# A hybrid RG-LRU and Gated DeltaNet step: one z tile's matmuls moved between front-stage steps, key loads and buffers rearranged, and a column group placed ahead of the RG-LRU gate products

## The reference, cut to what matters

```python
hn = rmsnorm(x, norm1)
xr, yr, qkv_raw, z, rest = jnp.split(hn @ w_in, SPLITS)
xc = causal_conv(xr) + rg_conv_b
gate_r = sigmoid(blockwise(xc, w_a) + b_a); gate_i = sigmoid(blockwise(xc, w_i) + b_i)
h = scan(a, sqrt(1 - a * a) * gate_i * xc)      # a from gate_r
out_rg = gelu(yr) * h
q, k, v = split(silu(causal_conv(qkv_raw)))      # q, k normalised
# per chunk of 128 tokens and head: A = 1 + strict(beta * k k^T * decay), solved for u, w
o, S = gated_delta_chunked(q, k, v, g, beta, S0)
out_gdn = rmsnorm(o, gdn_norm_w) * silu(z)
x = x + concat(out_rg, out_gdn) @ w_out
x = x + (silu(rms(x) @ w_gate) * (rms(x) @ w_up)) @ w_down
```

## Time and profile before

| | |
|---|---|
| median of 3 runs | 1476.22 us (1474.85 to 1478.69) |
| profiled execution: its time | 1474.63 us |
| its span in the trace | 1472.8 us |
| PE busy | 1416.4 us, 96% of the span |
| DVE, ACT, POOL busy | 42%, 25%, 11% |
| a q, k, v store of 512 KB, issue to landing (median) | 2.7 us |

### The profile page before, as it was taken

The page is one execution under the profiler, slowest core; times in us unless marked ns, Lnnn a source line. Parts: engine busy times, 40 slices in busy tenths (PEclk is TensorE's granted clock), DMA queues, the critical chain, the costliest instruction groups (busy, mean ns, idle before and its releaser), DMA issues.

```text
span 1472.8 us, 20785 instructions
## 1 busy us (share of the span) xinstructions
PE 1416.4 (96%) x8140; PEld 1299.6 (88%) x8140; DVE 625.5 (42%) x929; ACT 373.3 (25%) x612; POOL 158.6 (11%) x251
## 2 busy tenths in 40 slices
PE   6999999998898999999999999999999999999997
PEld 6888899997786899889898989898989898989895
DVE  6365455533352666643424242424242424242416
ACT  5345544332251222122020202020202020202012
POOL 3000000105474222210000000000000000000001
PEclk9999999997999999999999999999999999999999
DMA  6102211243544444327110101010101010100003
GB/s 224 62 18 75 75 69 74 100 145 133 194 173 126 140 129 126 123 99 283 54 58 29 57 28 57 28 57 28 57 28 57 28 57 28 57 28 28 0 0 121
DMA packets 66810, 119.93 MB, mean 81 GB/s; under 512 B 14672, under 2 KB 40208, under 8 KB 66768
## 3 DMA queue, kind: packets, MB, share of 16 engines
q1 hardware_dynamic: 66768, 119.36, 23.7%
HBM read 90.00 MB, written 29.34 MB: 81 GB/s over the span
## 4 chain that ended last, share of the span: by engine, by line
PE 46%; issue 2%; DMA 2%; ACT 2%; DVE 1%; SPq 0%; POOL 0%; ACTq 0%; DVEq 0%; POOLq 0%
PE bank L92 16%; PE bank L94 15%; PE bank L93 15%; ACT gu_hi L2060 1%; DMA gu_first_raw<-in_w_up 1%; DMA out_y<-y_out 1%; DVE acc L2146 0%; DVE y_out L2110 0%; DVE hf L2122 0%; ACT y_out L2096 0%; SPq L1987 0%; ACT gu_first_hi L2060 0%; SPq L1983 0%; POOL fstat L2161 0%; ACTq L81 0%
## 5 line engine op out<-in xcount | busy, mean ns | idle before, releaser
L92 PE MATMUL bank<-ht_hi,w_hi 128*128 128x364 f32 (+1 forms) x576 | 191.5, 332 | 0.0
L94 PE MATMUL bank<-ht_hi,w_lo 128*128 128x364 f32 (+1 forms) x576 | 189.9, 330 | 0.0
L93 PE MATMUL bank<-ht_lo,w_hi 128*128 128x364 f32 (+1 forms) x576 | 189.8, 330 | 0.0
L2122 DVE TENSOR_TENSOR hf<-sg,bank 128x364 f32<-128x364 f32 (+1 forms) x66 | 35.1, 532 | 338.6 <-PE bank L94 335.3
L92 PE MATMUL bank<-ht_hi,gu_hi 128*128 128x364 f32 (+1 forms) x528 | 173.2, 328 | 0.9 <-DVE hf L2122 0.9
L92 PE MATMUL bank<-ht_hi,gu_first_hi 128*128 128x364 f32 (+1 forms) x528 | 173.6, 329 | 0.5 <-PEq L930 0.5
L94 PE MATMUL bank<-ht_hi,gu_first_lo 128*128 128x364 f32 (+1 forms) x528 | 173.5, 329 | 0.0
L93 PE MATMUL bank<-ht_lo,gu_first_hi 128*128 128x364 f32 (+1 forms) x528 | 173.4, 328 | 0.0
L93 PE MATMUL bank<-ht_lo,gu_hi 128*128 128x364 f32 (+1 forms) x528 | 173.1, 328 | 0.0
L94 PE MATMUL bank<-ht_hi,gu_lo 128*128 128x364 f32 (+1 forms) x528 | 173.1, 328 | 0.0
L2146 DVE TENSOR_TENSOR acc<-acc,bank 128x512 f32<-128x512 f32 (+1 forms) x198 | 132.3, 685 | 90.3 <-PE bank L94 90.3
(11 more groups left out here) (297 smaller groups left out, 2213.5 us busy)
## 6 DMA issues: line engine op xcount, KB each, us to landing
w_raw<-in_w_in SPq DMA_DIRECT2D x24, 512.0 KB, 4.4
dn_raw<-in_w_down SPq DMA_DIRECT2D x22, 512.0 KB, 4.3
scratch_qkv<-cb_y SPq DMA_DIRECT2D x12, 512.0 KB, 2.7
scratch_kept<-kept SPq DMA_DIRECT2D x8, 768.0 KB, 3.7
gu_first_raw<-in_w_gate SPq DMA_DIRECT2D x11, 512.0 KB, 3.5
gu_first_raw<-in_w_up SPq DMA_DIRECT2D x11, 512.0 KB, 4.4
gu_raw<-in_w_gate SPq DMA_DIRECT2D x11, 512.0 KB, 3.5
gu_raw<-in_w_up SPq DMA_DIRECT2D x11, 512.0 KB, 4.4
```

Of the source, the lines that this page charges most:

```text
L92: pe.matmul(out, w_hi, x_hi, start=start, stop=False)
L93: pe.matmul(out, w_hi, x_lo, start=False, stop=False)
L94: return pe.matmul(out, w_lo, x_hi, start=False, stop=stop)
L2122: eng.tensor_tensor(hf[b][:, 0:m], sg[b][:, 0:m], psum[2 * b + 1][:, 0:m], ALU.mult).then_inc(hf_done, 1)
```

## The change

Five edits, in which TZ+1 is "the third z tile" by the new order of work.

1. PE projects only z tile TZ in the input block. Tile TZ+1 is made in the front stage, one step of three matmuls at a time (`z1_step`), at three places per front: ahead of `front`, behind it, and ahead of `products`. 24 steps fill fronts 0 to 7. Each of its three column groups uses bank 7; ACT copies it out (`keep_z1`) in fronts 2, 4 and 7, and the next group's first step waits for that copy. SP stores the row in front 7, and the load of `sub_u` waits for that store, because the row lies in the same memory. The samples' small products use bank 6 only.
2. At the end of the input block SP first waits for the last q, k, v stores and loads the keys, then the raw tiles TZ+2 and TZ+3. Their splits move into fronts 0 and 7 on ACT and DVE.
3. Three `kept` buffers instead of two.
4. In the RG-LRU loop, `project(2j+4, 0)` makes its first column group ahead of the gate products of j.
5. z is copied out of PSUM plain; the silu is applied when it is used (`silu_z`, one ACT operation per chunk).

```diff
@@ input_block, SP
             for s in range(2):
-                load_w(TZ + s, s)
-            for s in range(2):
                 eng.wait_ge(cb_out[s], 16 * PAIRS)
             for c in range(3):
                 eng.dma_start(k["qk_b"][c][:, :, :], ...).then_inc(q_ld[c], 16)
             for s in range(2):
-                eng.wait_ge(evac_done, TZ + s + 2)
-                eng.dma_start(scratch["z"][s], cb_y[s][:, 0:SEQ]).then_inc(z_out[s], 16)
+                load_w(TZ + s, s)
+            eng.wait_ge(evac_done, TZ + 2)
+            eng.dma_start(scratch["z"][0], cb_y[0][:, 0:SEQ]).then_inc(z_out[0], 16)
@@ input_block, PE
-            def project(t, s):
+            def project(t, s, groups=range(3)):
...
             def rg_tile(j):
-                project(2 * j + 2, 0)
+                first = isinstance(j, int) and j == 0
+                project(2 * j + 2, 0, range(0 if first else 1, 3))
...
                 project(2 * j + 3, 1)
+                project(2 * j + 4, 0, range(1))
...
-            with eng.Fori(1, PAIRS) as j:
-                two_tiles(TQ)(j)
-            two_tiles(TZ)(0)
+            project(TQ + 2, 0, range(1, 3))
+            project(TQ + 3, 1)
+            with eng.Fori(2, PAIRS) as j:
+                for s in range(2):
+                    project(TQ + 2 * j + s, s)
+            project(TZ, 0)
@@ mixer_block
+    z1_row = Plan(nc, gu_at + 4 * 4 * H * P)("z1_row", [P, SEQ])
-    kept = [B(f"kept{s}", [P, 3 * H, P]) for s in range(2)]
+    kept = [B(f"kept{s}", [P, 3 * H, P]) for s in range(3)]
@@ SP
+                if c == NC - 2:
+                    eng.wait_ge(m_["z_ev"], 4)
+                    eng.dma_start(scratch["z"][1], z1_row[:, :]).then_inc(z_out[1], 16)
                 if c == NC - 1:
+                    eng.wait_ge(z_out[1], 16)
...
@@ PE
+            def z1_step(n):
+                g, f = divmod(n, KT)
+                a, w = GROUPS[g]
+                if g and f == 0:
+                    eng.wait_ge(m_["z_ev"], g)
+                mm = mm3(eng, psum[7][:, 0:w], w_hi[1][:, f, :], ...)
...
             for f in FRONTS:
                 nxt = FRONTS[f.a + 1] if f.a + 1 < MT else None
+                z1_some(1)
                 if nxt:
                     front(nxt)
+                z1_some(1)
                 turn_k(f)
                 if nxt:
                     decay(nxt)
+                z1_some(1)
                 products(f)
@@ ACT
                 keep_kt(f)
                 if f.a == 0:
-                    eng.wait_ge(w_in1, 16 * W_TILES // 2)
-                    eng.activation(w_hi[1][:, :, :], w_raw1[:, :, :], ACT.Copy).then_inc(w_hi_done, 1)
+                    split_w(0)
+                if f.a in (2, 4, 7):
+                    keep_z1((2, 4, 7).index(f.a))
+                if f.a == 7:
+                    eng.wait_ge(m_["z_mm"], 3)
+                    split_w(1)
...
+            def silu_z(t):
...
+                eng.activation(t.z[:, :, 0:t.n], t.z[:, :, 0:t.n], ACT.Silu).then_inc(m_["z_done"], 1)
@@ DVE
                 if f.a == 0:
                     sample_start()
-                    eng.wait_ge(w_hi_done, W_TILES)
-                    eng.tensor_tensor(w_lo[1][:, :, :], ...)
+                    low_w(0)
+                if f.a == 7:
+                    low_w(1)
```

More of the change, by code:

```diff
@@ L387, in project @@
                 eng.wait_ge(evac_done, t)
-                for n, (a, m) in enumerate(GROUPS):
+                for n in groups:
+                    a, m = GROUPS[n]
                     for f in range(KT):
@@ L560, in _ @@
                 qkv(j)
[L562 to L570, removed]
+            eng.wait_ge(cb_out[0], 16 * PAIRS)
+            for n, (a, m) in enumerate(GROUPS):
+                e = min(a + m, SEQ)
+                eng.wait_ge(proj, 3 * TZ + n + 1)
+                eng.activation(cb_y[0][:, a:e], bank(0, n)[:, 0:e - a], ACT.Copy)
+            eng.activation(samp_z[:, 0, :], sample_bank(0), ACT.Copy).then_inc(evac_done, 1)
         @block.vector
@@ L771, in _ @@
                 two_rows(j)
-    return top, (w_raw[1], w_hi, w_lo), (w_in[1], w_hi_done, w_lo_done), z_out
+    return top, (w_raw, w_hi, w_lo), (w_in, w_hi_done, w_lo_done), z_out
 def mixer_block(nc, i, o, scratch, psum, B, k):
@@ L815, in mixer_block @@
     s_states = [normw[:, :].rearrange("p (b d) -> p b d", d=P)]
-    s_states += [Plan(nc, k["after_wo"] + 4 * D * s)(f"s_state{1 + s}", [P, NS, P])[:, :, :] for s in range(2)]
-    s_states += [B("s_state3", [P, NS, P])[:, :, :]]
+    s_states += [B("s_state1", [P, NS, P])[:, :, :]]
+    s_states += [Plan(nc, k["after_wo"] + 4 * D * s)(f"s_state{2 + s}", [P, NS, P])[:, :, :] for s in range(2)]
     wo_raw2 = B("wo_raw2", [P, D])
@@ L863, in __init__, with kept_count @@
                 self.qkv = qk_b[self.c % 3]
-                self.kn, self.u, self.mq = (kept[self.c % 2][:, q * H:(q + 1) * H, :] for q in range(3))
+                self.kn, self.u, self.mq = (kept[self.c % 3][:, q * H:(q + 1) * H, :] for q in range(3))
                 self.tle, self.ugt = tle, ugt
+    def kept_count(q):
+        return 80 * len(range(q, NC, 3))
     FRONTS = [Front(a) for a in range(MT)]
@@ L933, in _ @@
         def _(eng):
-            for h, sem in ((0, "ss_ld0"), (1, "ss_ld1")):
-                eng.dma_start(s_states[h], i["state_S"][h]).then_inc(m_[sem], 16)
+            for h in range(2):
+                eng.dma_start(s_states[h], i["state_S"][h]).then_inc(m_["ss_ld0"], 16)
             def load_wo(f):
@@ L1200, in project_z, with z1_some @@
                     mm.then_inc(m_["z_mm"], 1)
+            def z1_step(n):
[3 more added lines that the diff above has]
+                    eng.wait_ge(m_["z_ev"], g)
+                mm = mm3(eng, psum[7][:, 0:w], w_hi[1][:, f, :], w_lo[1][:, f, :],
+                         ht_hi[:, f, a:a + w], ht_lo[:, f, a:a + w], f == 0, f == KT - 1)
+                if f == KT - 1:
+                    mm.then_inc(m_["z_mm"], 1)
+            z1_steps = iter(range(3 * KT))
+            def z1_some(n):
+                for q in itertools.islice(z1_steps, n):
+                    z1_step(q)
             front(FRONTS[0])
@@ L1232, in project @@
                         if f == 0:
-                            eng.wait_ge(m_["z_ev"], 5 + half)
+                            eng.wait_ge(m_["z_ev"], 9 + half)
                     if (half, f) == (0, 0):
@@ L1519, in _ @@
             keep_z(1, range(3))
+            silu_z(Tile(NC))
             mix(Tile(NC))
@@ L1663, in mix @@
                 eng.wait_ge(m_["on_tr"], t.k + 1)
-                if not t.samples:
-                    eng.wait_ge(m_["z_ld"], 16 * t.k)
+                eng.wait_ge(m_["z_done"], t.k + 1)
                 eng.wait_ge(m_["init_done"], 1)
@@ L1695, in low_wo @@
                 if f == 0:
-                    eng.wait_ge(m_["kept_out1"], 80 * NC // 2)
+                    for q in range(3):
+                        eng.wait_ge(m_[f"kept_out{q}"], kept_count(q))
                 if f >= 6:
```

113 lines of the change are left out of this document (62 added, 51 removed).

## The result

| | before | after |
|---|---|---|
| median of 4 runs | 1476.70 us (1474.85 to 1478.69) | 1493.47 us (1491.76 to 1494.71) |
| profiled execution, its span | 1474.63, 1472.8 us | 1494.71, 1492.9 us |
| PE busy, mean granted clock | 1416.4 us, 0.985 | 1423.6 us, 0.977 |

The change makes the kernel slower by 16.8 us: ratio 1.0113, 95% interval 1.0095 to 1.0130.

The account below looks back on a forecast made before the run. PE was taken as the bound, busy for 96% of the span. Terms -12.0 + 8.7 + 5.7 + 5.5 + 5.7 + 1.0 + 0.5 = +15.1 on 1474.6 us gave 1489.7, stated as 1489, range 1468 to 1498.

Parts of the forecast that it names:

- z tile out of the input block: Input block: PE finishes last there, so moving one tile of 72 matmuls out saves 12.0 us.
- column group, with its clock: RG-LRU loop: PE waits for the low part before each early group, +8.7 us, plus +5.7 us of half speed.
- block change: End of input block: SP's held-up issue of six 512 KB transfers keeps PE at the barrier, +5.5 us.
- front stage, with its clock: Front stage: z steps fill waits, net +3.2; new waits for squares and copies bring it to +5.7 us, clock 0.
- POOL chain, late silu: POOL stretch after sub_u: z row's store is waited for, +1.0 us; extra ACT operation per chunk, +0.5 us.
- chain through the store and the load: RG-LRU loop: last tanh, vector chain, store, load, split, group, gates form a closed loop; rounds 32.45 us, were 29.65.
- I take 0: Front stage: no change in clock cost assumed, with bounds of -9 and +6 us.
- early return by which the sum was 1482: Front stage: by the skill's rule busy PE regains full clock soon, ending the stage some 7 us earlier, sum 1482.
- (a): RG-LRU loop and barrier: waits come but clock stays up and SP is through with PE; +0.5, about 1475 us; chance 0.17.
- (b): Front stage: dense z steps bring the clock back, -9 us on +0.5, 1466 us; chance 0.09.
- (c): RG-LRU loop: the group ahead does not stall and the gates' stalls go, 1460 us; chance 0.06.
- (d): Front stage: half speed throughout, +6 us more, and SP at the upper end, 1497 us; chance 0.08.

Follow-up runs that it names:

- the run with the early split: The change with raw tile 2j+6 requested before SP's wait for the row and DVE splitting tile 2j+4 ahead of the convolution: 1471.00 us, ratio 0.9973.
- the early raw tile alone: The change with only the raw tile requested early, DVE still splitting behind the convolution: 1486.31 us, ratio 1.0059.
- the run with the loads behind the barrier: The change with one key load ahead of the barrier, the other two key loads and both weight loads issued behind it: 1486.59 us, ratio 1.0073.
- the run with the weights first: The change with the two weight loads ahead of the key loads again, all five ahead of the barrier: 1492.17 us, ratio 1.0086.
- two kernels that leave it unchanged: The kernel before plus only the column group ahead, 1496.93 us; the kernel before plus only early raw request and split ahead of the convolution, 1479.34 us.
- the third group later: The change with early raw tile and split, loads behind the barrier, and front 5's third column group begun behind turn_k and the decay products: 1459.42 us, ratio 0.9880.
- the two kernels next to it: Both against the kernel at 1459.42 us: samples' first head spread behind the last front's squares, 1458.38 us; two kept buffers instead of three, 1459.85 us.
- the kernel with the samples spread later: The kernel at 1459.42 us with ACT spreading the samples' first head behind the last front's squares instead of ahead: 1458.38 us, ratio 0.9848.

## Why the prediction was right, and where its terms were off

The forecast was slower, 1489 us in a range of 1468 to 1498, for waits in the RG-LRU loop that eat the tile's 12 us, with the block change and the front stage losing on top. That is what happened, at 1493.5.

| term | predicted | in the profiled executions |
|---|---|---|
| z tile out of the input block | -12.0 | -12.0 |
| column group, with its clock | +14.4 | +15.2 |
| block change | +5.5 | +4.8 |
| front stage, with its clock | +5.7 | +10.7 |
| POOL chain, late silu | +1.5 | +0.2 |
| ahead of the loop, in unchanged work | 0 | +1.2 |
| sum | +15.1 | +20.1 |

The third column: the z tile is taken at 72 matmuls of 0.166 us; the block change is 6.25 - 1.43; the mixer's start moved from 328.74 to 337.89 us, +9.2, and less the other two terms and the 1.2 us that were there at 64.04 us, this leaves 15.2 for the loop; the front stage is 82.74 - 72.02; the POOL chain is what is left of 20.1. Some of the nearness of the sum is luck: the front stage came out 5.0 us dearer than said, the block change and the POOL chain 2.0 us cheaper, and the median rose by 16.8 us, not 20.1.

**The column group.** The mechanism, the four waits and their size (3 us, then 4 us) were read off one round of the kernel before, and the run with the early split shows them to be the cause. The later rounds, 34.3 us, are within 0.3 us of the 32.45 + 1.65 predicted. For j = 0, "the last tanh starts at 95.8", with 1.65 us of clock 97.4; it was 98.56, and less the 1.2 us by which this trace was late already, 97.4 as well. What the prediction left out is DVE's order. It is the whole cause in the first round, which the early raw tile alone leaves as it was, and the second branch of the loop in the others, which takes over as soon as the load is early. The prediction's chain through the store and the load holds for j = 1, 2, 3 only.

**The clock in the loop.** "Four waits of 3 to 4 us replace it": each has a stretch at 0.50 at it, of 3.4 us for the first, second and fourth, and of 6.8 us for the third (from 154.4, PE busy for 5.0 of them). That is what happened in this trace and no law: in the run with the early raw tile, waits of 2.5 and 2.7 us brought none.

**The block change.** SP's hold-up was rightly taken from the earlier trace rows, and the run with the loads behind the barrier gives the 4.8 us back. The working gave 6.7 us, and the 5.5 that was taken from it lay nearer. "Loading the keys first gains nothing" is borne out by the run with the weights first.

**The front stage** is the term that was mis-sized, in two steps. First, "they can fill the 8.8 us of waits". PE's idle time came off by 4.0 us (8.9 to 4.9), where I had 6.3: the waits of 1.5 us for `kept` and 0.7 us for `kt` lie in the last front, behind the 24th step, where no step is left to fill them, and the 0.9 us for the last squares I had not seen. Second, "I take 0" for the clock. PE's busy time rose by 14.7 us for 12.0 us of steps, so 2.7 us are half speed. The wait in front 5 came where I put it (1.56 us, predicted 1.9), but it brought 6.8 us at 0.50, which I had priced in the RG-LRU loop and not here. A doubt remains on the base of this term: the front stage of before took 72.0 us in its trace, and 77.3 and 77.2 us in those of two kernels that leave it unchanged.

**The rule of the skill.** The Trainium skill ("TensorE: Matmul & The Clock Gate", Part 1) says that activity releases a throttled clock. In after PE was busy for 14.3 of 17.0 us at 0.50, as it had been for 15.4 us in the earlier trace rows. The early return by which the sum was 1482 did not come at this place; at the RG-LRU waits, where dense groups follow, the stretches were of 3.4 us, one of 6.8.

**The rivals.** (a), nothing lost around the waits, is refuted by both clock rows and by the barrier. (b), dense z steps bring the clock back, is refuted for the change (0.83, as before) and is approached with the third group later: 0.95 in that kernel's fastest execution, 0.89 and 0.91 in the traces of the two kernels next to it. Fewer new waits go with it, though that they are the condition is not shown. (c), the group does not stall, failed for the reason given, and its mechanism is real: with the raw tile and the split early the group gains. (d), half speed throughout, did not come: between the stretches the clock is 1.00.

**A version that beats both.** Edit 4 with the raw tile and the split early, one key load ahead of the barrier, and the third column group behind `turn_k`: 1459.4 us, 1.2% below before (0.9864 to 0.9897) and 34 us below the change.

## What to carry to other kernels

Work that is put ahead of a stall has inputs of its own: before moving it, find when they are ready and what they hang on, since here they hung on the very chain whose stall it was to fill. When a loop is closed, list every branch that is within a few us of the longest, and shorten all of them in one experiment. And price a new wait with what the clock may do behind it: taking one of 1.6 us away gave 5.1 us, while two of 2.5 and 2.7 us in another kernel cost no clock at all.

## What the runs showed of the hardware

- A wait of 1.56 us in front 5 was followed by 6.8 us at 0.50 with PE busy for 6.72 of them; taking the wait away gave 5.1 us, three times its length.
- A wait need not bring half speed, and half speed needs no wait. In the kernel with the early raw tile alone, waits of 2.48 and 2.70 us left the granted clock at 1.00. In the kernel with the samples spread later, PE was busy for all of 20.9 us at 1.00 and then had 3.4 us at 0.51, while still busy:

```profile
336.20:357.10 20.90, 20.90 (x169) 1.00 0.58 196
357.10:360.50 3.40, 3.40 (x11) 0.51 0.97 361
```

- How long the half speed at the front stage's start lasts went with the idle time ahead of it only among the kernels with the z steps there: about 17 us in the five traces with 4.6 to 6.3 us of idle time at the barrier, and 10.2, 6.8, 3.4, 10.2 and 3.4 us in the five with 1.43. In the four without the steps the same 1.4 us was followed by about 17 us in two, before among them (the 15.4 us of the earlier trace rows are the inner part of it), and by about 10 us in the other two. So the idle time at the barrier is not the only cause. These are one execution each. Executions of one kernel differ too: of the version with the third group later three took 1459.3 to 1459.7 us and one 1454.5 us.
- SP's time to issue a transfer of 512 KB depended on what was under way: 0.4 us each for two weight loads behind small stores, and 4.61 us for the three key loads behind those; a key load that was first took 0.41 us.
